# Projections by tokens in chunks of four row blocks by 512 columns

## What is computed

```python
def hybrid_layer(x, ...):                       # first layer
    xn = rmsnorm(x, norm1_g[layer])
    u = xn @ w_in[layer].astype(f32)            # 1024 x 5632
    q_sb, k_sb, v_sb, f_raw, i_hg, q_hg, g_hg, gate_sb, gate_hg = jnp.split(u, list(c), axis=-1)
    ...                                         # v_sb, i_hg, g_hg: 512 columns each

def gla_mixer(h, w_in, w_gate_f, b_gate_f, w_gate_b, b_gate_b, g_out, w_out):
    q, k, v, r, zf, zb = split_cols(h @ w_in, [GLA_DK, GLA_DK, GLA_DV, GLA_DV, GLA_RANK, GLA_RANK])
    ...                                         # v, r: 1024 columns each
    o = rms_norm(o.transpose(0, 2, 1, 3).astype(h.dtype), g_out).reshape(bsz, seq, GLA_DV)
    return (o * jax.nn.silu(r)) @ w_out
```

## Time and profile before

| | us |
|---|---|
| median of 3 runs | 1089.12 |
| lowest, highest | 1088.84, 1090.90 |
| the profiled execution, its own time | 1090.03 |
| its span from first to last instruction | 1087.9 |

### The profile page before, as it was taken

The page is one execution under the profiler, slowest core; times in us unless marked ns, Lnnn a source line. Parts: engine busy times, 40 slices in busy tenths (PEclk is TensorE's granted clock), DMA queues, the critical chain, the costliest instruction groups (busy, mean ns, idle before and its releaser), DMA issues.

```text
span 1087.9 us, 18334 instructions
## 1 busy us (share of the span) xinstructions
PE 1068.6 (98%) x7750; PEld 1003.5 (92%) x7750; DVE 673.3 (62%) x759; ACT 575.6 (53%) x720; POOL 45.1 (4%) x51
## 2 busy tenths in 40 slices
PE   7999999999999999999999999999999999999998
PEld 7999999899999989998999999999998899999998
DVE  5557776665555565866655545567989665555454
ACT  6557544464434455755743444376676563434454
POOL 0000000020000010000103100010000100000010
PEclk9999999999999999999999999999999999999999
DMA  7835434546565655345456555545533455555551
GB/s 256 258 117 176 134 131 141 179 151 225 162 198 190 190 164 169 114 145 166 154 196 195 191 194 172 183 160 174 175 107 122 160 172 201 170 194 192 182 168 40
DMA packets 138305, 184.05 MB, mean 169 GB/s; under 512 B 4176, under 2 KB 122064, under 8 KB 138224
## 3 DMA queue, kind: packets, MB, share of 16 engines
q1 hardware_dynamic: 137776, 182.29, 51.4%
q0 software_dynamic: 160, 0.52, 0.1%
q10 hardware_dynamic: 288, 0.07, 0.0%
HBM read 181.82 MB, written 1.05 MB: 168 GB/s over the span
## 4 chain that ended last, share of the span: by engine, by line
PE 90%; DVE 3%; ACT 3%; DMA 2%; issue 1%; SPq 0%; ACTq 0%; DVEq 0%
PE PS L358 88%; PE PS L366 2%; ACT WH L1020 1%; DVE WL L1590 1%; DMA RAW<-in_w_in_dram 1%; DMA RAW<-in_gla_w_in_dram 1%; DMA H<-in_x_dram 0%; ACT HS L1035 0%; ACT AR L1035 0%; DVE SC L2173 0%; DVE HS L1679 0%; SPq L2385 0%; DVE AR L2111 0%; DVE H L2113 0%; DVE H L1648 0%
## 5 line engine op out<-in xcount | busy, mean ns | idle before, releaser
L1590 DVE TENSOR_TENSOR WL<-RAW,WH 128x2048 fp32r<-128x2048 f32 (+1 forms) x170 | 379.4, 2234 | 227.7 <-ACT WH L1020 227.2
L1020 ACT ACTIVATE WH<-RAW 128x2048 fp32r<-128x2048 f32 (+1 forms) x175 | 325.0, 1860 | 134.4 <-PE PS L358 127.2
L358 PE MATMUL PS<-OH,WH 128*128 128x256 f32 x744 | 212.1, 285 | 1.1 <-DVE AR L1978 1.1
L358 PE MATMUL PS<-WH,XH 128*128 128x256 f32 (+1 forms) x632 | 211.7, 335 | 0.3 <-ACT WH L1020 0.2
L358 PE MATMUL PS<-OL,WH 128*128 128x256 f32 x744 | 210.4, 283 | 0.0
L358 PE MATMUL PS<-OH,WL 128*128 128x256 f32 x744 | 210.4, 283 | 0.0
L358 PE MATMUL PS<-WL,XH 128*128 128x256 f32 (+1 forms) x632 | 208.8, 330 | 0.0
L358 PE MATMUL PS<-WH,XL 128*128 128x256 f32 (+1 forms) x632 | 208.5, 330 | 0.0
L358 PE MATMUL PS<-XH,WH 128*128 128x256 f32 x608 | 173.8, 286 | 1.5 <-DVE WL L1590 0.8
L358 PE MATMUL PS<-XL,WH 128*128 128x256 f32 x608 | 172.0, 283 | 0.0
L358 PE MATMUL PS<-XH,WL 128*128 128x256 f32 x608 | 172.0, 283 | 0.0
(11 more groups left out here) (201 smaller groups left out, 1144.6 us busy)
## 6 DMA issues: line engine op xcount, KB each, us to landing
RAW<-in_ffn_w_in_dram SPq DMA_DIRECT2D x44, 1024.0 KB, 5.1
RAW<-in_w_ff_dram SPq DMA_DIRECT2D x32, 1024.0 KB, 5.4
RAW<-in_ffn_w_out_dram SPq DMA_DIRECT2D x22, 1024.0 KB, 4.9
RAW<-in_w_in_dram SPq DMA_DIRECT2D x20, 1024.0 KB, 5.1
RAW<-in_gla_w_in_dram SPq DMA_DIRECT2D x12, 1024.0 KB, 5.5
RAW<-in_diff_w_in_dram SPq DMA_DIRECT2D x12, 1024.0 KB, 5.2
RAW<-in_ple_w_gate_dram SPq DMA_DIRECT2D x8, 1024.0 KB, 5.1
RAW<-in_w_out_dram SPq DMA_DIRECT2D x4, 1024.0 KB, 4.9
```

The source lines that it names most:

```text
L358: return e.matmul(o, l, r, start=start, stop=stop, skip_group_check=skip)
L1020: act(high, raw, ACT.Copy).then_inc(s["w_hi"], 1)
L1590: e.tensor_tensor(low, raw, high.bitcast(F32), ALU.subtract).then_inc(s["w_lo"], 1)
```

## The change

A third form of chunk, "long", is 4 row blocks by 512 columns, 1 MB as before; two of them (x = 0, 1) hold the 512 columns that two wide chunks held. `toks_long` works on one: for each token half, 4 row blocks by 3 matmuls of 128x512 into a bank of its own per token half. So a half is complete in the middle of the second chunk of a pair, where TensorE counts it in the new semaphore `long`, and the other at its end (`gemm`). All `toks` chunks of the first layer and GLA and the first two gate chunks of each layer become long ones, 18 in all; differential attention's stay. Copies out of PSUM take one token half of 512 columns each. Banks, and the waits for them, change accordingly.

```diff
+    long = lambda name, n0: out.extend((name, 4 * x, 4, n0, 512) for x in range(2))
...
-    return {"ohg": (6, 7), "gl0": (1, 6, 2, 3), "gl1": (6, 4, 5, 7), "nm0": (0, 1, 2, 3),
+    return {"ohg": (6, 7), "gl0": (0, 1, 2, 3), "nm0": (0, 1, 2, 3),
...
+LONG = {4: (4, 7), 5: (4, 7), 10: (7, 0), 11: (7, 0), 12: (1, 7), 13: (1, 7)}
+GLA_LONG = ((4, 5), (0, 1), (7, 0), (6, 7))
...
         if name == "nm1":
-            e.wait_ge(s["ple_h"], k // 2 + 1)
+            e.wait_ge(s["ple_h"], max(k // 2 + 1, 2))
...
+    def toks_long(c, x, banks, ops, halves=(0, 1), norm=None, free=None):
+        w = m.weights(c)
+        if halves[0] == 0:
+            ready(c)
+        for tb in halves:
+            if x == 0 and free:
+                free(tb)
+            for k in range(4):
+                if norm and tb == 0:
+                    ahead(norm, 4 * x + k)
+                i = mm3(PS[:, banks[tb], :], [y[:, 4 * x + k, tb * 128:tb * 128 + 128] for y in ops],
+                        [y[:, k, :] for y in w], x == 0 and k == 0, x == 1 and k == 3)
+            if x == 1 and tb == 0:
+                i.then_inc(s["long"], 1)
+        if halves[-1] == 1:
+            i.then_inc(s["gemm"], 1)
...
# TensorE, ple(layer)
-            toks(AT[f"ple_w_gate{layer}"] + n, 3 + n, m.pair("OX"[layer]), f"pn{layer}" if n == 0 else None)
-            if layer == 0 and n >= 1:
-                h_step("nm1", 2 * n - 2)
-                h_step("nm1", 2 * n - 1)
+        toks_long(c, 0, (3, 4), ops, (0, 1), f"pn{layer}")
+        e.wait_ge(s["res"], r0)
+        toks_long(c + 1, 1, (3, 4), ops, (0, 1), f"pn{layer}")
+        toks(c + 2, 5, ops, None, range(4))
+        if layer == 0:
+            h_step("nm1", 0)
+            h_step("nm1", 1)
+        toks(c + 2, 5, ops, None, range(4, 8))
+        if layer == 0:
+            h_step("nm1", 2)
+            h_step("nm1", 3)
+        toks(c + 3, 6, ops)
+        if layer == 0:
+            h_step("nm1", 4)
+            h_step("nm1", 5)
...
# ScalarE, first layer, evac(n)
+        if n in LONG:
+            if j == 0:
+                e.wait_ge(s["long"], (4, 10, 12).index(n) + 1)
+            else:
+                e.wait_ge(s["gemm"], c + 1)
+            act(v3({2: v, 5: GS, 6: vh}[i], 2)[:, j, :], PS[:, LONG[n][j], :], ACT.Copy).then_inc(s["win_ev"], 1)
+            return
...
# ScalarE, GLA, evac(n)
-        e.wait_ge(s["gemm"], c0 + n + 2)
+        if tb:
+            e.wait_ge(s["gemm"], c0 + n + 2)
+        else:
+            e.wait_ge(s["long"], 4 + j)
...
# ScalarE, ple(layer)
+            if n == 1:
+                for tb in range(2):
+                    e.wait_ge(*((s["gemm"], c + 2) if tb else (s["long"], 8 + layer)))
+                    act(g[:, tb, 0:512], PS[:, 3 + tb, :], ACT.Sigmoid, scale=r[:, tb:tb + 1]).then_inc(s["ple_g"], 1)
+                continue
...
-            if layer == 0 and n >= 1:
-                turn_hi("nm1", 2 * n - 2, 2 * n - 1)
+            if layer == 0 and n == 2:
+                turn_hi("nm1", 0, 1, 2, 3)
...
# VectorE, ple(layer)
+            if layer == 0 and n == 2:
+                turn_lo("nm1", 0, 1, 2, 3)
+            elif layer == 0 and n == 3:
+                turn_lo("nm1", 4, 5)
...
# SyncE, output
-        e.wait_ge(s["ple_h"], 5 + n)
+        e.wait_ge(s["ple_h"], max(5 + n, 6))
```

More of the change, by code:

```diff
@@ L85, in weight_chunks @@
             tall("w_ff2", i - 1)
-    for i in range(12):
+    for i in range(4):
         wide("gla_w_in", 256 * i)
@@ L89, in weight_chunks @@
             wide("gla_w_in", 3072, 32)
+    for i in range(2, 6):
+        long("gla_w_in", 512 * i)
     for i in range(4):
@@ L105, in weight_chunks @@
                 tall(f"ffn_w_out{layer}", i - 1)
-        for i in range(4):
+        long(f"ple_w_gate{layer}", 0)
+        for i in range(2, 4):
             wide(f"ple_w_gate{layer}", 256 * i)
@@ L679, in tensor_program, with gin, free @@
     c0 = AT["gla_w_in"]
-    def gin(n, ks=range(8)):
-        if ks[0] == 0 and 3 <= n < 6:
-            e.wait_ge(s["gl_qk"], n - 1)
-        elif ks[0] == 0 and 6 <= n < 11:
-            e.wait_ge(s["gla_ev"], n - 5)
-        if n < 4:
-            feat(c0 + n + (n >= 2), n % 2 if n else 4, m.pair("O"), None if n else "nm0", ks)
-        else:
-            toks(c0 + n + 1, n % 2 if n < 11 else 7, m.pair("O"), None, ks)
+    def gin(n, halves=(0, 1)):
+        if n < 4:
+            if n == 3:
+                e.wait_ge(s["gl_qk"], 2)
+            feat(c0 + n + (n >= 2), n % 2 if n else 4, m.pair("O"), None if n else "nm0", range(4 * halves[0], 4 * halves[-1] + 4))
+            return
+        j = n // 2 - 2
+        def free(tb):
+            if j < 2:
+                e.wait_ge(s["gl_qk"], ((1, 1), (3, 4))[j][tb])
+            elif j == 2:
+                e.wait_ge(*((s["gla_ev"], 3) if tb else (s["gl_m"], 2)))
+            else:
+                e.wait_ge(*((s["gla_ev"], 5) if tb else (s["gl_x"], 4)))
+        toks_long(c0 + n + 1, n % 2, GLA_LONG[j], m.pair("O"), halves, None, free)
     def low_rank():
@@ L732, in tensor_program @@
     low_rank()
-    gin(2, range(4))
+    gin(2, (0,))
     spread_r("nm0", 7)
-    gin(2, range(4, 8))
+    gin(2, (1,))
     gin(3)
@@ L742, in tensor_program @@
         gin(n)
-    gin(8, range(4))
+    gin(8, (0,))
     e.wait_ge(s["gl_z"], 5)
@@ L769, in tensor_program @@
     i.then_inc(s["gl_s"], 1)
-    gin(8, range(4, 8))
+    gin(8, (1,))
     e.wait_ge(s["gl_w"], 1)
@@ L835, in ple @@
         r0 = 16 if layer == 0 else 24
-        for n in range(4):
-            if n == 1:
-                e.wait_ge(s["res"], r0)
-            toks(AT[f"ple_w_gate{layer}"] + n, 3 + n, m.pair("OX"[layer]), f"pn{layer}" if n == 0 else None)
-            if layer == 0 and n >= 1:
-                h_step("nm1", 2 * n - 2)
-                h_step("nm1", 2 * n - 1)
+        c, ops = AT[f"ple_w_gate{layer}"], m.pair("OX"[layer])
+        toks_long(c, 0, (3, 4), ops, (0, 1), f"pn{layer}")
[13 more added lines that the diff above has]
+            h_step("nm1", 5)
     swiglu(0)
@@ L1179, in scalar_program @@
     sigmoid(fr, fr)
+    sigmoid(E_[0], qh)
+    hi(w0 + 13)
     evac(10)
-    hi(w0 + 13)
-    sigmoid(E_[0], qh)
     evac(11)
@@ L1286, in evac @@
     def evac(n):
[L1288 to L1292 removed]
+        j, tb = n // 2 - 2, n % 2
+        if tb:
+            e.wait_ge(s["gemm"], c0 + n + 2)
+        else:
+            e.wait_ge(s["long"], 4 + j)
+        act(v3(gv if j < 2 else gr, 2)[:, tb, 512 * (j % 2):512 * (j % 2) + 512], PS[:, GLA_LONG[j][tb], :],
+            ACT.Copy if j < 3 else ACT.Silu, scale=rr[:, tb:tb + 1]).then_inc(s["gla_ev"], 1)
     def softplus(d):
@@ L2105, in ple @@
         for n in range(4):
-            c = slice(256 * n, 256 * n + 256)
             lo(AT[f"ple_w_gate{layer}"] + n + 2)
-            gg = v3(g, 2)[:, :, c]
-            e.wait_ge(s["ple_pw"], 4 * layer + 4)
+            if n == 0:
+                e.wait_ge(s["ple_pw"], 4 * layer + 4)
+            tb, c = (slice(n, n + 1), slice(0, 512)) if n < 2 else (slice(0, 2), slice(256 * n, 256 * n + 256))
+            gg = v3(g, 2)[:, tb, c]
             e.wait_ge(s["ple_g"], 4 * layer + n + 1)
-            e.tensor_tensor(gg, gg, v3(pw, 2)[:, :, c], ALU.mult).then_inc(own.up(), 1)
+            e.tensor_tensor(gg, gg, v3(pw, 2)[:, tb, c], ALU.mult).then_inc(own.up(), 1)
             settled()
-            e.tensor_tensor(H[:, :, c], H[:, :, c], gg, ALU.add).then_inc(s["ple_h"], 1)
-            if layer == 0 and n >= 1:
-                turn_lo("nm1", 2 * n - 2, 2 * n - 1)
+            e.tensor_tensor(H[:, tb, c], H[:, tb, c], gg, ALU.add).then_inc(s["ple_h"], 1)
+            if layer == 0 and n == 2:
+                turn_lo("nm1", 0, 1, 2, 3)
+            elif layer == 0 and n == 3:
+                turn_lo("nm1", 4, 5)
     ple(0, swiglu(0))
```

47 lines of the change are left out of this document (27 added, 20 removed).

## The result

| | before | after |
|---|---|---|
| median of 6 runs each, us | 1090.01 | 1100.39 |
| lowest, highest, us | 1087.60, 1091.71 | 1097.48, 1103.46 |
| the profiled execution, its own time, us | 1090.03 | 1097.48 |
| its span, us | 1087.9 | 1095.2 |

The ratio of after to before is 1.0094, 95% interval [1.0076, 1.0112]: slower by 0.9%. The forecast was 1096.9 us, with a range of 1092 to 1100.5. The profiled execution was 7.3 us longer in its span; the sum had said 7.75. The median moved by more, 10.4 us. So there are two results to explain: where the 7.3 us come from, and where the 3 us on top of it in the median.

A forecast was written before the change was run, and what follows sets the result against it. TensorE's own issue time plus few stalls was taken as the bound. Terms -1.65 + 0 + 1.3 + 6.25 + 1.85 = +7.75 us took the span from 1087.9 to 1095.7, the median from 1089.12 to 1096.9 us; range 1092 to 1100.5.

The forecast's parts named there:

- first layer: First layer's long chunks: 1.8 us gained by fewer matmuls, 0.15 us lost at the pair scores' wait, net -1.65 us.
- GLA, up to the scores: GLA before its scores: 1.35 us gained, then TensorE waits 1.3 us on VectorE's products, net 0.
- GLA, rest: GLA's norm and turn: TensorE waits 2.3 us before turning blocks, last pair half gives 0.3 back, net +1.3 us.
- gates, layer 0: Embeddings' gate stage of layer 0: three new TensorE waits, (a), (b) and (c), net +6.25 us.
- (a): Gate stage: block 7 transposed later, so the third gate chunk's weight split is late; 2.2 us wait in layer 0.
- (b): Layer 0 gates: blocks 0 and 1 of the next norm need both sums of the pair; 1.9 us wait.
- (c): Layer 0 gates: block 3 of the next norm waits for block 0's bank, turned late by VectorE; 2.9 us.
- gates, layer 1: Embeddings' gate stage of layer 1: only (a) applies, net +1.85 us.
- Rival 4: A wide matmul is worth two narrow ones, so no gain: 5.4 us more, 1102.3 us; 3%.
- Rivals 2 and 3: rival 2; and waits only match the gain: 1092.1 us without (b), (c) (7%), about 1088.5 without GLA's too (5%).
- rival 2: ScalarE gets the first token half early, hiding the waits; only the gain is left: 1083.7 us, faster; 6%.
- rival 1: Clock falls after TensorE's new stalls, some 1.5 us each, one to three of them: 1098.4 to 1101.4 us; 16%.

The follow-up runs named there:

- third experiment: Changed kernel with block 7 of the gates' norm transposed ahead of the first long chunk's second token half, not behind it; 1094.46 us.
- fourth: Changed kernel with GLA's third values copy moved behind the exponentials and its fifth copy behind the squares and inverse roots, on ScalarE; 1096.01 us.
- sixth: Changed kernel with all six late results moved by order: block 7 earlier, next norm's turns later, GLA's two copies later; 1087.02 us.
- ninth: The sixth's kernel with ScalarE's two row squares of the next norm moved behind the fourth gate chunk's sigmoid; 1084.99 us.
- seventh: Changed kernel with only the gate stages mended: block 7 turned earlier, next norm's blocks turned later, GLA left as changed; 1091.13 us.
- eleventh: The tenth's kernel with one unused ScalarE square ahead of the split of layer 1's third gate chunk, for a short wait; 1086.55 us.
- twelfth: The tenth's kernel with two unused ScalarE squares ahead of the split of layer 1's third gate chunk, for a long wait; 1088.16 us.
- last four experiments: The ninth, tenth, eleventh and twelfth, each timed beside the kernel before; 1084.99, 1085.96, 1086.55 and 1088.16 us.
- tenth: Repeat: changed kernel with the embeddings' gates as before the change and GLA's two copies moved behind what they held up; 1085.96 us.
- fifth: Changed kernel with every 128x512 matmul of the long chunks issued as two of 128x256; 1103.43 us.

## Why the prediction was right, and where it wasn't

Starts of TensorE in the profile after against those of before, in the order of the sum:

| step | forecast, us | profile, us | read from |
|---|---|---|---|
| first layer | -1.65 | -1.7 | block turned at 404.23, now 402.51 |
| GLA, up to the scores | 0 | -0.5 | 466.26, now 464.03, less the step above |
| wait at the scores | 1.3 | 1.43 | |
| GLA, rest | +1.3 | +1.6 | the next turn of H, 520.34 before, now 519.69 |
| wait at the turn | 2.3 | 2.40 | |
| gates, layer 0 | +6.25 | +6.2 | first scores of differential attention, 773.23 before, now 778.78 |
| its waits (a), (b), (c) | 2.2, 1.9, 2.9 | 2.08, 1.80, 2.65 | |
| gates, layer 1 | +1.85 | +1.75 | the rest of the span |
| its wait | 2.3 | 2.10 | |
| sum | +7.75 | +7.3 | |

**Right, and shown.** All six waits came where they were forecast, released by what was forecast, each within 0.25 us. That each has the cause that the sum names is shown by taking it away: the turn of block 7 (third experiment), the two copies in GLA (fourth), the turns of the next norm (sixth and ninth; the wait that came in their place is down to 0.77 us in the ninth). The gain per matmul is 12.9 ns at full clock where the sum had 12.6. Rival 4 fell with the narrow matmuls. Rivals 2 and 3 fell with the first profile: for rival 2, the early half did not help, since what ScalarE needs first stands behind a later event in its list. The Trainium skill's page TensorE: Matmul & The Clock Gate, section "Wait — 56ns, not 53.3ns?", has 2.5 ns as the fixed cost of a warm matmul; the rows here disagree, with five times that for these fp32r matmuls.

**Too small a term.** "Wider rows in a weight transfer may land earlier or later by some tenths" was held to -0.4 to +0.4 and set to 0. It was -0.69. Before the change, at the fourth chunk of GLA, the splits on ScalarE wait for a transfer and TensorE for VectorE behind them. Before, then after:

```profile
423.50 1.91 ACT L1020 ACTIVATE WH<-RAW 128x2048 fp32r<-128x2048 f32 x1 [2.44 <-DMA RAW<-in_gla_w_in_dram]
...
429.06 0.38 PE L358 MATMUL PS<-OH,WH 128*128 128x256 f32 x1 [1.11 <-DVE AR L1978]
```

```profile
421.09 1.92 ACT L1072 ACTIVATE WH<-RAW 128x2048 fp32r<-128x2048 f32 x1 [1.75 <-DMA RAW<-in_gla_w_in_dram]
...
426.66 0.38 PE L370 MATMUL PS<-OH,WH 128*128 128x256 f32 x1 [0.42 <-DVE AR L2047]
```

The wait for the transfer is 0.69 us shorter and TensorE's is 0.69 shorter with it. The transfers of these weights took 5.5 us from issue to landing in the median before, 5.2 after. All later versions, all with long chunks in GLA, have TensorE's wait at 0.24 to 0.59 us. That it is the longer rows which land sooner is argued from this, not isolated; against it, the transfers of the first layer's and of the gates' weights, 6 of 20 and 4 of 8 of which got the longer rows, took 5.1 us in the median before and after.

**The step that failed: the price of the clock, and its chance.** The forecast put the median at the sum, and gave 16% to rival 1, "the clock falls after the new stalls", at 1.5 us a fall and one to three of them, 1098.4 to 1101.4 us. The median of 1100.39 lies there, outside the forecast's own spread of 1094 to 1099. It is inside the range by 0.1 us, and that is luck: the range took in most of a rival that the forecast held to be unlikely.

Of the 3.5 us between 1096.9 and 1100.39, 0.9 lies in the start: the median of the kernel before was 1089.12 in three executions and 1090.01 in six. The sum was 0.45 too high. The rest, 3 us, goes with a lower clock: 0.993 and 0.992 in four of the six executions. The price of a fall was right where nothing follows it, 1.49 us; the fourth experiment shows one that cost nothing. The chance was wrong, and the argument against the rival was the mistake: "the longest stall of TensorE on VectorE today is 1.80 us, with no lower clock behind it". For that very stall, at 404, it holds: none of the fourteen profiles has a fall there. But it says little of other stalls. In four profiles (the sixth, seventh, eleventh and twelfth experiments) the clock did fall behind the wait of 1.8 us at 184, which the kernel before has as well (186.38). "Shorter than any behind which this trace shows a fall" was no argument either: up to the last matmul the only fall in that trace stands behind GLA's low-rank gates, and behind no stall at all. A fall is an event that some executions have and others don't. Of the waits of 1.8 us or more that the changed kernel and the experiments added, 25 over all profiles, 9 have a fall right behind them; each of the changed kernel's five places is among them in the profile of some version, none in its own two. (In the fourth experiment the clock was already low when the wait ended.)

How uneven executions are, the kernel before shows. Its 24 executions beside the last four experiments are 5 at 1087.6 to 1088.1 us (clock 0.999), 7 at 1088.8 to 1089.4 (0.998) and 12 at 1091.1 to 1092.1 (0.996 or 0.997). So one profile and three times said little on the clock. The sign that the prediction named for the rival, a mean clock below 0.99, could not have shown it: the longest execution, 1104.33 us, has 0.992.

What ties the lower clock to the waits: every lower stretch found in the fourteen profiles, up to the last matmul, stands right behind GLA's low-rank gates or right behind a wait of 1.79 us or more, and one wait of 2.0 us added to a kernel cost 0.7 us more than itself in the mean, one of 0.9 us nothing more. The spread of the executions proves little. It is 0.6 us in the ninth experiment, 0.9 in the tenth, 3.0 with the one long wait added and 6.0 and 6.4 for the changed kernel; but it is 1.0 in the fourth, which has three of the new waits left, and 4.4 in the 24 executions of the kernel before, which has no more long waits than the tenth. The Trainium skill's same page, section "Why this matters for your kernels", says that long idle gaps between bursts of matmuls bring the lower clock back; the rows agree, and show it at gaps as short as 1.79 us.

What stays open: how many falls a given execution has. Only profiled executions can be looked into, and no profile of the changed kernel was of a long execution. That its longer executions have more falls, and that these sit behind the new waits, is argued from the mean clocks and the other versions' profiles, not shown. The number is open too: an estimate from the fourth experiment, where two falls go with a mean clock 0.003 lower, gives about three falls more for the executions at 0.993 and four for those at 0.992. Three at 1.49 us would be 4.5 us, where the executions at 0.993 are 3 us longer; a fall that the next wait takes up would fit, and isn't shown.

## What to carry over

When a result is regrouped so that it comes complete later but in larger pieces, walk the queue of the engine that reads it, and move its reading instruction behind everything that doesn't need it; here the order of five instruction groups was worth 1.3%, and the matmuls saved 0.5%. Ahead of such a move, count what it puts ahead of the next needed instruction too: the squares behind a turn that was moved later made a new wait of 2 us. And take a wait of TensorE of 2 us for more than 2 us, here for 2.7 in the mean: price it with the clock behind it, by several executions and not by one profile.

## What the hardware showed

- Of TensorE's two clock levels 2.4 GHz is granted nearly always (0.995 to 0.998 in the mean of the fourteen profiled executions). Falls to 1.2 GHz (a granted clock of 0.50 from 1070 to 1072 us in the twelfth experiment) came behind idle times of 1.79 to 2.65 us: in 9 of the 25 cases that the change or an edit brought, and in 4 of 14 at the wait of 184. They came behind none of 1.43 us or less; nothing between was measured. The wait of 1.8 us at 404, in all fourteen profiles, had none behind it. Behind GLA's low-rank gates the granted clock from 436 to 440 us was 0.57 to 0.84 in ten profiles and 1.00 in four (the fifth, sixth, seventh and twelfth experiments); that fall costs 1.2 us.
- A fall costs nothing where the next wait takes it up: in the fourth experiment it shortened (b) from 1.80 to 0.35 us, and block 3 came no later.
- The wait of 1.8 us at 184 brought a fall in the four profiles in which TensorE's first turned block of that place came at 180.06 to 180.33 us, and none in those with 180.8 to 182.5 us. The program around it is the same; what differs is when it comes.
- With no wait behind it, one fall costs 1.49 us in 96 matmuls of 256 columns.
- The start of the kernel differs between executions: TensorE's first attention scores come between 39.6 and 41.1 us. Spans that differ by under 1.5 us are better compared by stages.
